# A two-layer encoder on one core: heads turned between the attention products, and half of the gated addition of rows 2 and 3 on GpSimd

## The chip, the cores and the metric

The program runs on one core of one Trainium2 chip. The metric is the device time of one execution in microseconds, the median over runs. The kernel before takes 1689.68 us (three runs, 1689.37 to 1691.24). Everything is fp32.

## The reference

Two sequences of 256 tokens (prompt and sample), 1024 wide, go through two layers and a last norm. Layer 0 mixes with latent attention, layer 1 with a gated delta rule in both directions (GDN). Both layers then have a mixture of 16 experts and a gate stage, and that stage's sum is what the next norm reads:

```python
def encoder_trunk(x, p, W):
    h = x
    for i in range(DEPTH):
        hn = rmsnorm(h, W['norm_mix_g'][i])
        j = i // N_MIXERS
        if i % N_MIXERS == 0:
            h = h + mla_mixer(hn, ...)
        else:
            h = h + gdn_mixer(hn, ...)
        h = h + expert_choice_moe(rmsnorm(h, W['norm_ffn_g'][i]), ...)
        gate = jax.nn.sigmoid(rmsnorm(h, W['norm_ple_g'][i]) @ W['ple_w_gate'][i])
        h = h + (p[i] @ W['ple_w_proj'][i]) * gate
    return rmsnorm(h, W['final_norm_g'])

def gdn_mixer(h, ...):
    ...
    o = (o_fwd + o_bwd).astype(h.dtype)
    o = rmsnorm(o, norm_g) * jax.nn.silu(z.reshape(B, S, H, GDN_DV))
    return o.reshape(B, S, H * GDN_DV) @ w_out
```

## The kernel before

The 512 tokens lie in four rows of 128 (row 0 and 1: prompt, 2 and 3: sample), kept in SBUF as `h[:, row, :]`. Each engine has one instruction stream, written by hand and worked off in order; semaphores tie the streams together. So the order of the work is the order of the code, and a wait holds back all that stands behind it on its engine.

**The gate stage**, once per layer. TensorE makes seven block products (P1, P2, P6, P5, P3, P7, P4 in this order, two row halves `t` each), from which four quarters of the product with the gate weights are put together by a scheme with seven instead of eight products. VectorE adds the products as they come out of PSUM (`gate_add`, line 3033). ScalarE takes the sigmoid of each 128x512 block (`sigmoid`, line 1456). Then the block is multiplied by the projection `pp` (line 3042) and added to `h` (line 3043): the function `gated_add(j, f)`, for row j and half f. `PLE_ORDER` fixes the eight blocks: (0,0), (1,0), (0,1), (1,1), (2,1), (3,1), (2,0), (3,0); `ple_sig` counts sigmoids, `ple_added` counts additions, both in this order. Rows 0 and 1 are done before P7; rows 2 and 3 close the stage. In `norm_quarters` ScalarE squares each half once it is added (line 951), adds a small constant (line 959), loads another table, and takes the roots (line 964); VectorE takes the reciprocal (2307) and scales (2314 in layer 0, 2310 in layer 1, where the output leaves by DMA); in layer 0 ScalarE scales the other half (line 972), and TensorE turns the rows (line 1489) for the next projection. On ScalarE the sigmoid of (2,0) stands behind the squares of (2,1), and the sigmoid of (3,0) behind the squares of (3,1) and (2,0).

**GpSimd in the gate stage** (`ple_pool`) makes sums of weight blocks for the products, four instructions of 128x2048 (lines 819, 821, 822, 825). In layer 0 the next thing in its stream is `gdn_pool`: `weight_sums(0)`, four instructions of 128x1024 on line 842 that need only weights loaded long before, and that TensorE reads after its first product of the GDN projection; then sums over the turned tokens (855, 857), which wait for TensorE and the copies out of PSUM.

**The end of the GDN mixer.** In the loop over quarters the last pass (p == QS) has on TensorE `new_values` (line 1780), `turn_heads(0)` (line 1927: heads 0 to 3 of the gated output turned, once VectorE's `gate_out(0, 2)` and `(0, 3)`, line 2777, are done), and four `attend` (line 1780), whose results VectorE adds (`add_av`, line 2766). The read of the last one frees the slots into which SyncE loads the first expert weights of layer 1 (line 662). Then come the output products (line 1499) and `turn_heads(1)`, which waits for the gated heads 4 to 7. The product P2 waits for heads 5 and 7 copied out by VectorE (line 2873).

Of the kernel before, what the change touches and what calls it, by code (L numbers as in the profile page):

```python
# [16 lines left out]
ALU = mybir.AluOpType  # L17
# [3 lines left out]
D = 1024  # L21
# [5 lines left out]
NT = SEQ // P  # L27
# [32 lines left out]
QS = 4  # L60
# [97 lines left out]
def trunk_kernel(nc, x_prompt, x_sample, p_prompt, p_sample, norm_mix_g, norm_ffn_g, norm_ple_g,  # L158
# [4 lines left out]
    with ExitStack() as ctx:  # L163
# [583 lines left out]
        def _(pool):  # L747
# [63 lines left out]
            def ple_pool(l):  # L811

                b11, b12, b21, b22 = pg_w_in(l)
                t1, t2 = pg_t(l)
                pool.wait_ge(moe_sem["w_used"], NPIECE * (l + 1))
                for f in range(2):
                    wait_use(pool, f"ple_g{f}{l}")
                pool.wait_ge(mo_tokens, PLE_TOKENS[l] + 2)
                pool.tensor_tensor(t1, b12, b11, ALU.subtract).then_inc(mo_weights, 1)  # L819
                pool.wait_ge(mo_weights, PLE_WEIGHTS[l] + 1)  # L820
                pool.tensor_tensor(t2, b22, t1, ALU.subtract).then_inc(mo_weights, 1)
                pool.tensor_tensor(b12, b22, b12, ALU.subtract).then_inc(mo_weights, 1)
                pool.wait_ge(mo_weights, PLE_WEIGHTS[l] + 3)
                pool.wait_ge(*lay[l].s_pg.full(out_no(P2, 1) + 1))
                pool.tensor_tensor(b21, b21, t2, ALU.subtract).then_inc(mo_weights, 1)

            ple_pool(0)

# [633 lines left out]
        def _(pe):  # L1462
# [209 lines left out]
            def gdn_pe():  # L1672
# [266 lines left out]
                for p in range(QS + 1):  # L1939
# [72 lines left out]
                    if live:  # L2012
                        level_turn(p, 3)
                        level_z(p, 4)
                    if p == QS:
                        turn_heads(0)
                    if p:
                        for a in range(4):
                            attend(prev, a)
                    else:  # L2020
                        gate_part(7, 5, KD)
# [273 lines left out]
        def _(dve):  # L2295
# [599 lines left out]
            for l in LAYERS:  # L2895
# [141 lines left out]
                def gated_add(j, f):  # L3037
# [2 lines left out]
                    dve.wait_ge(ple_sig, n)  # L3040
                    b, hv = ple_block(j, f), h[:, j, f * HALF:(f + 1) * HALF]
                    link(dve.tensor_tensor(b, b, pp(l)[:, j, f * HALF:(f + 1) * HALF], ALU.mult))
                    dve.tensor_tensor(hv, hv, b, ALU.add).then_inc(ple_added, 1)

                L.s_pxt.wait_read(dve, KD - 1)
# [26 lines left out]
                for t in range(NT):  # L3072
# [1 line left out]
                    gate_add(pg_q[:, t, :], pg_q[:, t, :], P7, t)  # L3074
                    dve.wait_ge(ple_added, 8 * l + 3 + t)
                    norm(normed, t)
                for t in range(NT):
                    gated_add(NT + t, 1)
                    if t == 0:
                        dve.wait_ge(*L.s_pg.freed(out_no(P7, 1)))  # L3080
                        gate_add(pg_q[:, 0, :], pg_q[:, 0, :], P4, 0)
                gated_add(NT, 0)
                gate_add(pg_q[:, 1, :], pg_q[:, 1, :], P4, 1)
                gated_add(NT + 1, 0)
# [30 lines left out]
```

## Time and profile before

| | |
|---|---|
| median of three runs | 1689.68 us |
| the profiled execution | 1692.57 us, of it span 1690.8 us |
| granted TensorE clock over the span | 0.984 |
| TensorE busy | 1590.7 us (94%) |
| VectorE, ScalarE, GpSimd busy | 674.0, 439.2, 203.6 us |
| chain that ended last | TensorE 68%, DMA 12%, VectorE 12%, ScalarE 6% |
| gate stage, layer 0 | 653.58 us to 710.26 us |
| gate stage, layer 1, with the last norm | 1631.92 us to the end |

The profile is one execution. A timeline has one row for a run of like instructions on an engine: where it starts, how long it lasts from the first start to the last end, and in brackets how long the engine was idle before it and what it was released by. An instruction's duration contains the time in which it was begun but held up. PE is TensorE, DVE VectorE, ACT ScalarE, POOL GpSimd, SP SyncE. `banks` is PSUM; `ring`, `misc`, `work`, `h`, `xn`, `xt` lie in SBUF.

### The profile page before, as it was taken

What the parts mean: (1) busy time and instruction counts of PE and PEld (TensorE: products, weight loads), DVE (VectorE), ACT (ScalarE), POOL (GpSimd) and SP (SyncE); (2) the same over time, 40 slices, a digit from 0 to 9 for tenths busy, and PEclk for the clock granted to TensorE, in tenths of its full rate; (3) what the DMA queues carried; (4) which work ended last, traced back from release to release, by engine and by line L of the source; (5) the groups of instructions that cost most, each with busy time, mean ns of one, the idle gap of its engine ahead of it and who ended that gap; (6) DMA issues with size and microseconds to landing.
All of it is one profiled execution on the core that took longest, in us unless ns stands there. A gap on an engine that the chain in (4) does not pass through costs nothing.

```text
span 1690.8 us, 21260 instructions
## 1 busy us (share of the span) xinstructions
PE 1590.7 (94%) x8950; PEld 823.3 (49%) x8950; DVE 674.0 (40%) x1130; ACT 439.2 (26%) x972; POOL 203.6 (12%) x120
## 2 busy tenths in 40 slices
PE   8989899999989978899999999998999999999887
PEld 4464534343343324488875688854344433433233
DVE  3564411131210215789983466684111312102056
ACT  4332301101101003422125765533111010110043
POOL 2302000000000004353402211130000000000021
PEclk9999999999999999999999999999999999999999
DMA  8104699999999995012121110276899999999941
GB/s 288 74 27 173 270 423 422 397 428 427 428 424 428 428 424 213 0 51 101 50 100 50 27 27 2 101 298 249 366 425 410 428 428 428 423 428 429 426 184 50
DMA packets 54045, 454.56 MB, mean 269 GB/s; under 512 B 5187, under 2 KB 7519, under 8 KB 28991
## 3 DMA queue, kind: packets, MB, share of 16 engines
q1 hardware_dynamic: 53424, 452.90, 65.3%
q8 instruction: 71, 1.16, 0.3%
q0 software_dynamic: 288, 0.22, 0.0%
q14 instruction: 23, 0.19, 0.0%
q10 hardware_dynamic: 239, 0.09, 0.0%
HBM read 451.07 MB, written 2.13 MB: 268 GB/s over the span
## 4 chain that ended last, share of the span: by engine, by line
PE 68%; DMA 12%; DVE 12%; ACT 6%; issue 2%; DVEq 0%; SPq 0%; ACTq 0%
PE banks L2151 31%; PE banks L1499 12%; DMA ring<-in_moe_w_down 7%; PE banks L2122 4%; DVE misc L2575 4%; PE banks L1682 3%; DMA ring<-in_moe_w_up 3%; PE banks L1780 3%; PE banks L2184 3%; PE banks L2212 2%; PE banks L1745 2%; DMA ring<-in_moe_w_gate 1%; PE banks L1607 1%; DVE misc L2573 1%; PE banks L2160 1%
## 5 line engine op out<-in xcount | busy, mean ns | idle before, releaser
L2151 PE MATMUL banks<-ring,misc 128*64 128x512 f32 x1984 | 442.6, 597 | 10.7 <-DMA ring<-in_moe_w_up 5.7
L2151 PEld LDWEIGHTS banks<-ring,misc 128*64 128x64 f32 x1984 | 138.7, 137 | 285.2 <-issue 266.1
L2151 PE MATMUL banks<-ring,hid_t 128*64 128x512 f32 x960 | 217.2, 605 | 14.4 <-DMA ring<-in_moe_w_down 14.3
L2999 DVE TENSOR_TENSOR work<-work,banks 128x512 f32<-128x512 f32 x32 | 33.7, 1052 | 439.9 <-PE banks L2151 439.9
L1438 ACT ACTIVATE misc<-banks 32x512 f32<-32x512 f32 x64 | 37.5, 586 | 417.2 <-PE banks L2151 416.8
L2151 PEld LDWEIGHTS banks<-ring,hid_t 128*64 128x64 f32 x960 | 69.1, 139 | 152.8 <-issue 144.0
L3014 DVE COPY misc<-banks 32x512 f32<-32x512 f32 x64 | 44.2, 691 | 229.5 <-PE banks L2151 229.1
L819 POOL TENSOR_TENSOR ring<-ring 128x2048 f32<-128x2048 f32 x2 | 10.9, 5454 | 995.0 <-DVE ring L3050 995.0
L1499 PE MATMUL banks<-ring,xt 128*128 128x512 f32 (+1 forms) x280 | 118.9, 583 | 0.2
L2575 DVE SCALAR_TENSOR_TENSOR misc<-ring,conv_w,misc 128x512 f32<-128x512 f32 x96 | 93.8, 977 | 3.4
L1682 PE MATMUL banks<-ring 128*128 128x256 f32 x384 | 86.0, 380 | 0.0
L1499 PEld LDWEIGHTS banks<-ring,xt 128*128 128x128 f32 x280 | 53.0, 190 | 63.6 <-issue 63.1
L1682 PEld LDWEIGHTS banks<-ring 128*128 128x128 f32 x384 | 72.4, 190 | 13.0 <-DVE ring L2507 3.4
L1424 ACT ACTIVATE work<-banks 128x512 f32<-128x512 f32 x32 | 19.1, 597 | 211.7 <-PE banks L2151 211.7
L842 POOL TENSOR_TENSOR ring<-ring 128x1024 f32<-128x1024 f32 x24 | 61.3, 2555 | 67.6 <-PE banks L1682 66.6
L2184 PE MATMUL banks<-misc,xt 128*128 128x512 f32 x128 | 61.8, 618 | 4.8 <-DVE misc L3014 3.4
L1682 PE MATMUL banks<-xt,ring 128*128 128x256 f32 x288 | 64.5, 380 | 0.0
L2122 PEld LDWEIGHTS banks<-xt,xn 128*128 128x128 f32 x512 | 59.5, 196 | 8.9 <-issue 6.5
L2122 PE MATMUL banks<-xt,xn 128*128 128x128 f32 x512 | 61.4, 281 | 2.2 <-DVE xt L2940 2.2
L1682 PEld LDWEIGHTS banks<-xt,ring 128*128 128x128 f32 x288 | 54.6, 190 | 7.5 <-issue 0.2
L1745 PE MATMUL banks<-ring,xt 128*128 128x512 f32 x128 | 57.5, 598 | 0.0
L1780 PE MATMUL banks<-ring 128*128 128x128 f32 x384 | 49.2, 280 | 3.9 <-DVE ring L2669 1.6
(389 smaller groups left out, 1940.0 us busy)
## 6 DMA issues: line engine op xcount, KB each, us to landing
ring<-in_moe_w_gate SPq DMA_DIRECT2D x62, 2048.0 KB, 15.5
ring<-in_moe_w_up SPq DMA_DIRECT2D x62, 2048.0 KB, 18.3
ring<-in_moe_w_down SPq DMA_DIRECT2D x56, 2048.0 KB, 19.5
ring<-in_gdn_w_in SPq DMA_DIRECT2D x8, 2048.0 KB, 8.9
ring<-in_ple_w_gate SPq DMA_DIRECT2D x4, 2048.0 KB, 16.5
ring<-in_moe_w_down SPq DMA_DIRECT2D x6, 1024.0 KB, 23.4
ring<-in_mla_w_out SPq DMA_DIRECT2D x2, 2048.0 KB, 24.3
misc<-in_moe_w_down SPq DMA_DIRECT2D x2, 2048.0 KB, 15.1
```

The costliest lines, as they stand in the source:

```text
L842: pool.tensor_tensor(out, x, y, op).then_inc(w_comb_done, 1)
L1438: ins = act.activation(ybuf[32 * i:32 * i + 32, s, 0:HALF], psum[32 * s:32 * s + 32, down_bank(ex - 1), :], ACT.Copy)
L1499: mm = pe.matmul(psum[:, banks.bank(st, i), 0:cols], lhs(k), rhs(k), start=(k == 0), stop=(k == n - 1))
L1682: mm = pe.matmul(psum[:, b, 256 * m:256 * m + 256], lhs[:, k, P * m:P * m + P], rhs[:, k, :], start=(k == 0), stop=(k == 3))
L1745: mm = pe.matmul(psum[:, apply_banks.bank(s_z, i), :], xt[:, k, j * P:(j + 1) * P], slot(6 + f, KD, HALF)[:, k, :], start=(k == 0), stop=( ...
L1780: mm = pe.matmul(o, lhs(g), rhs(g), start=True, stop=True)
L2122: mm = pe.matmul(o, xn[:, NT * s + t, c0:c0 + P], oh[:, q, NT * s + t, :], start=(t == 0), stop=(t == NT - 1))
L2151: mm = pe.matmul(psum[64 * f:64 * f + 64, bank, :], tokens(4 * kh + k), row(k, f), start=(kh == 0 and k == 0), stop=(kh == 1 and k == 3))
L2184: pe.matmul(psum[:, scatter_bank(q, g), :], sc[:, q, j, :], ybuf[:, j // NT, f * HALF:(f + 1) * HALF], start=True, stop=True).then_inc(moe ...
L2212: mm = pe.matmul(psum[:, b, :], ptt(l)[:, k, j * P:(j + 1) * P], w_proj(l)[:, k, f * HALF:(f + 1) * HALF], start=(k == 0), stop=(k == 1))
L2575: ins = dve.scalar_tensor_tensor(out=a, in0=x, scalar=w, in1=a, op0=ALU.mult, op1=ALU.add)
L3014: ins = dve.tensor_copy(ybuf[32 * i:32 * i + 32, s, HALF:D], psum[64 + 32 * s:96 + 32 * s, down_bank(ex - 1), :])
```

## The change

Two edits. First, `gated_add(2, 1)` and `gated_add(3, 1)` go from VectorE to GpSimd, in both layers, with the same arithmetic: GpSimd's multiplication waits for the sigmoid, its addition for the `ple_added` count, and VectorE's addition of (2,0) now waits until both have been counted. They are put at the end of `ple_pool`, so in layer 0 ahead of `weight_sums(0)`. On VectorE the addition of P4's first half, which stood between the two, now follows P7's norms. Second, `turn_heads(0)` goes from ahead of the four `attend` to between the second and the third.

```diff
--- before.py
+++ after.py
@@ -823,6 +823,13 @@
                 pool.wait_ge(mo_weights, PLE_WEIGHTS[l] + 3)
                 pool.wait_ge(*lay[l].s_pg.full(out_no(P2, 1) + 1))
                 pool.tensor_tensor(b21, b21, t2, ALU.subtract).then_inc(mo_weights, 1)
+                for t in range(NT):
+                    n = PLE_ORDER.index((NT + t, 1)) + 8 * l
+                    b, hv = ple_block(NT + t, 1), h[:, NT + t, HALF:D]
+                    pool.wait_ge(ple_sig, n + 1)
+                    link(pool.tensor_tensor(b, b, pp(l)[:, NT + t, HALF:D], ALU.mult))
+                    pool.wait_ge(ple_added, n)
+                    pool.tensor_tensor(hv, hv, b, ALU.add).then_inc(ple_added, 1)
 
             ple_pool(0)
 
@@ -2012,10 +2019,10 @@
                     if live:
                         level_turn(p, 3)
                         level_z(p, 4)
-                    if p == QS:
-                        turn_heads(0)
                     if p:
                         for a in range(4):
+                            if p == QS and a == 2:
+                                turn_heads(0)
                             attend(prev, a)
                     else:
                         gate_part(7, 5, KD)
@@ -3040,6 +3047,8 @@
                     dve.wait_ge(ple_sig, n)
                     b, hv = ple_block(j, f), h[:, j, f * HALF:(f + 1) * HALF]
                     link(dve.tensor_tensor(b, b, pp(l)[:, j, f * HALF:(f + 1) * HALF], ALU.mult))
+                    if (j, f) == (NT, 0):
+                        dve.wait_ge(ple_added, n - 1)
                     dve.tensor_tensor(hv, hv, b, ALU.add).then_inc(ple_added, 1)
 
                 L.s_pxt.wait_read(dve, KD - 1)
@@ -3074,11 +3083,8 @@
                     gate_add(pg_q[:, t, :], pg_q[:, t, :], P7, t)
                     dve.wait_ge(ple_added, 8 * l + 3 + t)
                     norm(normed, t)
-                for t in range(NT):
-                    gated_add(NT + t, 1)
-                    if t == 0:
-                        dve.wait_ge(*L.s_pg.freed(out_no(P7, 1)))
-                        gate_add(pg_q[:, 0, :], pg_q[:, 0, :], P4, 0)
+                dve.wait_ge(*L.s_pg.freed(out_no(P7, 1)))
+                gate_add(pg_q[:, 0, :], pg_q[:, 0, :], P4, 0)
                 gated_add(NT, 0)
                 gate_add(pg_q[:, 1, :], pg_q[:, 1, :], P4, 1)
                 gated_add(NT + 1, 0)
```

GpSimd's stream before, from the last weight sum of layer 0's gate stage on (`weight_sums` and `token_sums_dve` are counters, `slot6_loaded` is the arrival of the first GDN weights):

```order
L825 TENSOR_TENSOR ring<-ring 128x2048 [waits xt_in_psum,out_weight_sums]
L842 TENSOR_TENSOR ring<-ring 128x1024 [waits slot6_loaded,w_used]
L842 TENSOR_TENSOR ring<-ring 128x1024 [waits weight_sums] x2
L842 TENSOR_TENSOR ring<-ring 128x1024
L855 TENSOR_TENSOR ring<-xt 128x1024 [waits xt_read_dve,xt_read_act]
```

And with the change:

```order
L825 TENSOR_TENSOR ring<-ring 128x2048 [waits xt_in_psum,out_weight_sums]
L830 TENSOR_TENSOR misc<-misc,ring 128x512 [waits ple_sigmoid]
L832 TENSOR_TENSOR h<-h,misc 128x512 [waits ple_added,pool_link]
L830 TENSOR_TENSOR misc<-misc,ring 128x512 [waits ple_sigmoid]
L832 TENSOR_TENSOR h<-h,misc 128x512 [waits ple_added,pool_link]
L849 TENSOR_TENSOR ring<-ring 128x1024 [waits slot6_loaded,w_used]
L849 TENSOR_TENSOR ring<-ring 128x1024 [waits weight_sums] x2
L849 TENSOR_TENSOR ring<-ring 128x1024
L862 TENSOR_TENSOR ring<-xt 128x1024 [waits xt_read_dve,xt_read_act]
```

The four weight sums (842, now 849) stand behind four new instructions, of which the first waits for a sigmoid late in the stage.

VectorE's stream before, from the additions of P7's second half to the end of layer 0's gate stage (3033 reads PSUM, 3042 and 3043 are a gated addition):

```order
L3042 TENSOR_TENSOR misc<-misc,ring 128x512 [waits ple_sigmoid]
L3043 TENSOR_TENSOR h<-h,misc 128x512 [waits dve_link]
L3033 TENSOR_TENSOR misc<-misc,banks 128x512 [waits xt_in_psum,xt_read_dve]
L3042 TENSOR_TENSOR misc<-misc,ring 128x512 [waits ple_sigmoid]
L3043 TENSOR_TENSOR h<-h,misc 128x512 [waits dve_link]
L3042 TENSOR_TENSOR misc<-misc,ring 128x512 [waits ple_sigmoid]
L3043 TENSOR_TENSOR h<-h,misc 128x512 [waits dve_link]
L3033 TENSOR_TENSOR misc<-misc,banks 128x512 [waits xt_in_psum]
L3042 TENSOR_TENSOR misc<-misc,ring 128x512 [waits ple_sigmoid]
L3043 TENSOR_TENSOR h<-h,misc 128x512 [waits dve_link]
L2307 RECIPROCAL rstd<-rms 128x1 [waits sq_done,ple_added]
L2314 TENSOR_SCALAR xn<-h,rstd 128x512 [waits rstd_done]
```

And with the change:

```order
L3040 TENSOR_TENSOR misc<-misc,banks 128x512 [waits xt_in_psum,xt_read_dve]
L3049 TENSOR_TENSOR misc<-misc,ring 128x512 [waits ple_sigmoid]
L3052 TENSOR_TENSOR h<-h,misc 128x512 [waits ple_added,dve_link]
L3040 TENSOR_TENSOR misc<-misc,banks 128x512 [waits xt_in_psum]
L3049 TENSOR_TENSOR misc<-misc,ring 128x512 [waits ple_sigmoid]
L3052 TENSOR_TENSOR h<-h,misc 128x512 [waits dve_link]
L2314 RECIPROCAL rstd<-rms 128x1 [waits sq_done,ple_added]
L2321 TENSOR_SCALAR xn<-h,rstd 128x512 [waits rstd_done]
```

Two multiplications and two additions are gone from VectorE, and one addition has a wait more. (Lines behind the new code count seven to nine higher.)

TensorE's stream before, from the last `new_values` to the last `attend` (the rows on `misc,ring` are `attend`):

```order
L1780 MATMUL banks<-ring 128x128 [waits core_vn_read_act,gdn_ba_read_dve,core_du6_read_dve]
L1780 MATMUL banks<-ring 128x128 x3
L1927 MATMUL banks<-ident,xn 128x128 [waits gated]
L1927 MATMUL banks<-ident,xn 128x128 x15
L1780 MATMUL banks<-misc,ring 128x128 [waits core_vn_read_act,gdn_ba_t_read_dve]
L1780 MATMUL banks<-misc,ring 128x128 x3
```

And with the change:

```order
L1787 MATMUL banks<-misc,ring 128x128 [waits core_vn_read_act,gdn_ba_t_read_dve]
L1787 MATMUL banks<-misc,ring 128x128 x3
L1934 MATMUL banks<-ident,xn 128x128 [waits gated]
L1934 MATMUL banks<-ident,xn 128x128 x15
L1787 MATMUL banks<-misc,ring 128x128 [waits core_vn_read_act,gdn_ba_t_read_dve]
L1787 MATMUL banks<-misc,ring 128x128 x3
L1787 MATMUL banks<-misc,ring 128x128 [waits core_av_read_dve,gdn_ba_t_read_dve,core_vn_read_act]
L1787 MATMUL banks<-misc,ring 128x128 x3
```

The wait for the gated heads now has two `attend` less behind it. The streams of ScalarE and SyncE have the same instructions as before.

## Rows read from the trace of the kernel before

**Rows 1.** The page, part 1: busy time of each engine, and share of the span.

```profile
PE 1590.7 (94%) x8950; PEld 823.3 (49%) x8950; DVE 674.0 (40%) x1130; ACT 439.2 (26%) x972; POOL 203.6 (12%) x120
```

**Rows 2.** Timeline of VectorE, layer 0's gate: start, us, engine, line, operation, names, shapes, idle before.

```profile
676.23 2.64 DVE L3042 TENSOR_TENSOR misc<-misc,ring 128x512 f32<-128x512 f32 x1
...
684.42 2.72 DVE L3043 TENSOR_TENSOR h<-h,misc 128x512 f32<-128x512 f32 x1
...
696.93 1.28 DVE L3033 TENSOR_TENSOR misc<-misc,banks 128x512 f32<-128x512 f32 x2
...
701.01 0.69 DVE L3042 TENSOR_TENSOR misc<-misc,ring 128x512 f32<-128x512 f32 x1 [2.21 <-ACT misc L1456]
...
708.96 0.49 DVE L2314 TENSOR_SCALAR xn<-h,rstd 128x512 f32<-128x512 f32 x1
```

**Rows 3.** Timeline of GpSimd, the same stage.

```profile
672.93 5.39 POOL L825 TENSOR_TENSOR ring<-ring 128x2048 f32<-128x2048 f32 x1
678.27 11.10 POOL L842 TENSOR_TENSOR ring<-ring 128x1024 f32<-128x1024 f32 x4
```

**Rows 4.** Timeline of ScalarE, the same stage, its last part.

```profile
700.35 1.15 ACT L1456 ACTIVATE misc<-misc 128x512 f32<-128x512 f32 x2
702.46 0.63 ACT L951 ACTIVATE work<-h 128x512 f32<-128x512 f32 x1 [0.96 <-DVE h L3043]
...
703.42 0.61 ACT L1456 ACTIVATE misc<-misc 128x512 f32<-128x512 f32 x1
...
708.56 0.61 ACT L951 ACTIVATE work<-h 128x512 f32<-128x512 f32 x1
...
709.50 1.32 ACT L972 ACTIVATE xn<-h,rstd 128x512 f32<-128x512 f32 x2
```

**Rows 5.** Timeline of TensorE, the same stage.

```profile
682.29 20.76 PE L1499 MATMUL banks<-ring,xt 128*128 128x512 f32 x48
...
710.26 1.97 PE L1489 MATMUL banks<-ident,xn 128*128 128x128 f32 x8 [3.49 <-ACT xn L972]
```

**Rows 6.** Timeline of VectorE, layer 1's gate.

```profile
1675.96 1.28 DVE L2310 SCALAR_TENSOR_TENSOR xn<-h,rstd,misc 128x1024 f32<-128x1024 f32 x1
...
1681.75 0.68 DVE L3033 TENSOR_TENSOR misc<-misc,banks 128x512 f32<-128x512 f32 x1
```

**Rows 7.** Timeline of ScalarE, layer 1's gate.

```profile
1674.53 0.63 ACT L1456 ACTIVATE misc<-misc 128x512 f32<-128x512 f32 x1
...
1679.57 0.61 ACT L1456 ACTIVATE misc<-misc 128x512 f32<-128x512 f32 x1
```

**Rows 8.** Groups by line on GpSimd: count, busy us, mean ns, idle before.

```profile
L842 POOL TENSOR_TENSOR ring<-ring 128x1024 f32<-128x1024 f32 x24 | 61.3, 2555 | 67.6 <-PE banks L1682 66.6
...
L807 POOL TENSOR_TENSOR h<-h,misc 128x512 f32<-128x512 f32 x4 | 5.0, 1262 | 5.0 <-DVE misc L2450 5.0
```

**Rows 9.** Chain of waits, around the turned heads: start, us, what.

```profile
1098.34 4.74 DVE xn L2777 x8
...
1103.12 1.97 PE banks L1927 x16
1105.09 3.57 PE banks L1780 x32
...
1120.71 3.44 PE banks L1499 x8
```

**Rows 10.** Timeline of VectorE, around the turned heads.

```profile
1109.51 4.70 DVE L2777 SCALAR_TENSOR_TENSOR xn<-xn,fac,ring 128x128 f32<-128x128 f32 x4
...
1122.70 1.40 DVE L2873 TENSOR_SCALAR misc<-banks,gains 128x512 f32<-128x512 f32 x2
```

**Rows 11.** Timeline of SyncE: a weight load of layer 1's experts.

```profile
1145.07 0.33 SPq L662 DMA_DIRECT2D ring<-in_moe_w_up  x1
```

**Rows 12.** Busy us in stretches, granted clock (PEclk), DMA share and GB/s.

```profile
710.00:714.00 4.00, 3.74 (x36) 3.57 (x40) 1.69 (x3) 2.34 (x5) 0.00 (x0) 0.61 0.00 0
...
1200.00:1300.00 100.00, 99.08 (x508) 41.73 (x506) 15.38 (x26) 11.56 (x22) 0.00 (x0) 0.98 1.00 420
```

## The prediction

> **What bounds the kernel now.** I read the page's busy times first: TensorE has work for 1590.7 of 1690.8 us [rows 1], so an edit counts only where TensorE stands still, or at the very end. Three such places are touched: the end of layer 0's gate stage, the turned heads, and the last norm. I read the timeline of each engine at each of them.
>
> At the end of layer 0's gate stage TensorE is through with its products at 682.29 + 20.76 = 703.05 and starts on the rest of the turned rows only at 710.26, after an idle time put down to ScalarE [rows 5]. Between lies a chain of ScalarE and VectorE: sigmoids, gated additions, squares, roots, scaling.
>
> The decisive reading is what a GpSimd instruction does to VectorE. A gated multiplication or addition on VectorE takes 0.69 us where GpSimd is idle (701.01), and 2.64 and 2.72 us beside GpSimd's weight sums (676.23, 684.42) [rows 2]. It isn't slower work, it is waiting: the instruction of 676.23 ends at 678.87, just behind GpSimd's line 825, which ends at 678.32; and then four instructions of line 842 take 11.10 us while four of VectorE pass, so the two engines alternate in cycles of 2.78 us, some 0.68 for VectorE and 2.1 for GpSimd [rows 2, 3]. The Trainium skill states this as a rule: in "SBUF — State Buffer", section "SBUF: two separate sides", GpSimd and a VectorE instruction with two SBUF inputs take a port pair as an exclusive lock for the whole instruction, and the other is fully blocked. The trace agrees (2.64 against 0.69 us). The rule speaks against moving work to GpSimd beside a critical VectorE; that the waiting engine has its turn before the other's next instruction only the trace shows. Were the load merely shared, as the same page's section "A bandwidth-pool intuition that's wrong (but worth ruling out)" rejects, the delay would be that of my second rival.
>
> **Part 1, layer 0's gate stage.** In the kernel before, the four weight sums of line 842 run from 678.27 to 689.37 [rows 3], where VectorE has slack: the products set the pace. With the change they stand behind GpSimd's four new instructions, and these wait for a sigmoid at about 700. So the sums fall into the chain at the end. Step by step:
>
> 1. Relief early. VectorE, no longer held up at 678 to 687, gets to P7's second half when TensorE delivers it: fourth of six products in 20.76 us, so 682.29 + 4 x 3.46 = 696.13, instead of 696.93 [rows 2, 5]. Some 0.7 us. The two sigmoids of 700.35 [rows 4] start at 699.65, the first ends at about 700.3.
> 2. GpSimd's own four instructions: 128x512 additions took 1.26 us each there [rows 8]; a multiplication of that shape I take as the same. With two short hand-overs, 5.2 us: 700.35 to 705.55. The first addition ends at 702.95.
> 3. ScalarE squares (2,1) then; from the start of that square to the next sigmoid are 703.42 - 702.46 = 0.96 us [rows 4], so the sigmoid of (2,0) runs 703.95 to 704.55. Its multiplication on VectorE finds GpSimd in its fourth instruction and runs 705.6 to 706.25.
> 4. The weight sums start now. From 706.25 GpSimd and VectorE alternate: sum 1, addition of (2,0) (ends 709.0); sum 2, multiplication of (3,0) (ends 711.8, its sigmoid came at about 710.5); sum 3, addition of (3,0) (ends 714.6); sum 4 to 716.7; then the scaling of row 2, 0.49 us [rows 2], to 717.2. Before, that scaling ended at 708.96 + 0.49 = 709.45. ScalarE's part, from the square of (3,0) to its scaling 709.50 - 708.56 = 0.94 us [rows 4], fits beneath sum 4 (714.7 to 715.7).
> 5. TensorE starts on row 2 at 717.25 instead of 710.26: **+7.0 us**. It is not given back: the next stage begins with this turn. Nor does the lateness of the sums hurt there, since they end at 716.7 and TensorE needs them only after the rest of the turn and the first product.
>
> I haven't seen a GpSimd gated addition or a lock dispute over the scaling in this place; from both sides: if VectorE never lost its turn, the 0.7 gained in step 1 and the 0.5 lost in steps 2 and 3 leave -1 to +1; if it met one more cycle at each end, +9. I take 7.0, since the alternation is measured four times over.
>
> TensorE's clock: behind the 3.49 us of idle the granted clock was 0.61 over 710 to 714, so mostly at 1.2 instead of 2.4 GHz [rows 5, 12]. The idle grows to about 10.5 us. I take the same loss behind it; were it to last as long again, +1.6 us (4 x 0.39, all of it lost once more).
>
> **Part 2, the turned heads.** TensorE waits for VectorE's gating (which itself waits behind GpSimd: 4.74 us for eight small instructions) until 1103.12, with four `attend` queued behind, in the row that follows the turn, 3.57 us [rows 9]. Two of them, half of it or 1.8 us, now fill that gap. But what is late next? TensorE's product P2 starts when the turned heads 5 and 7 are copied: VectorE ends that at 1122.70 + 1.40 = 1124.10, and TensorE's own work ends at 1120.71 + 3.44 = 1124.15 [rows 9, 10]. The two are level before. So TensorE's 1.8 us is worth only what VectorE's chain gains, and that is held by GpSimd's line 911, which stretches four gatings at 1109.51 to 4.70 us [rows 10]; that instruction comes behind another on GpSimd that doesn't move, so VectorE's end moves little. I take **-0.3 us**, between 0 and -1.9. The expert weights, freed by the last `attend`, are asked for some 1.6 us earlier; it brings nothing, as five of them, 2 MB each at some 420 GB/s [rows 12], are through by about 1135, and the next load waits for an output product until 1145.07 [rows 11].
>
> From there the shift goes through one to one: the weight stream runs at full share only from 1200 on [rows 12], and what starts it is TensorE's first release of a slot.
>
> **Part 3, layer 1's gate stage and the last norm.** No weight sums follow here, only the four new instructions. GpSimd's first runs 1675.2 to 1676.45 behind the sigmoid of 1674.53 [rows 7]; VectorE's scaling of row 1, at 1675.96 [rows 6], waits for it and ends at 1677.7 (+0.4); GpSimd's addition waits in turn and ends at 1678.85, and its second pair at 1681.35. The sigmoid of (2,0), 1679.57 before [rows 7], starts at 1679.8; its multiplication waits for the lock until 1681.35, its addition ends at 1682.65, and P4's second half, 1681.75 before [rows 6], is added at 1682.6. All that follows hangs on it: **+0.9 us**, between -0.3 (P4's second half, added as soon as TensorE allows, which I put at 1681.4) and +2.
>
> **Sum.** 7.0 - 0.3 + 0.9 = +7.6 us. The profiled execution, 1692.57 us (span 1690.8), would become 1700.2. The median of the runs shown is 2.9 us lower; 1689.68 + 7.6 = **1697.3 us**, with 1695 to 1699.5 as this case's own range. From no change a measurement here can tell about 0.2%, or 3.4 us.
>
> **Rivals.**
> - *The gate is delayed further* (0.12): the alternation meets more VectorE instructions, or the low clock behind the longer idle lasts. +9 or +7.6 + 1.6, near 1699.5 to 1701.
> - *Little dispute at the end* (0.14): the weight sums fall into gaps where VectorE waits for ScalarE anyway. For: VectorE itself waits there for ScalarE, 2.21 us before 701.01 [rows 2]. Against: cycles of 2.78 us four times running. It costs 1 to 3 us, 1691 to 1692.5.
> - *Faster* (0.05): the lock falls to VectorE at each of its requests at 705 to 717, and VectorE's gating of the heads also comes out ahead of line 911. Then the early relief (-0.7) and two `attend` in TensorE's gap (-1.9) remain, -0.3 at the end: 1689.68 - 2.9 = 1686.8. It decides for this case if VectorE's gated additions keep 0.69 us at the end of layer 0's stage. Against it stands that GpSimd's instruction, once begun, wasn't interrupted anywhere in rows 2 and 3.
> - The forecast: 0.69.
>
> Eight times in ten: 1692.0 to 1700.5. Faster by over 0.2% is a part of the third rival alone, 0.03; slower by over 0.2% (above 1693.1) is the forecast and the first rival, and a little of the second, 0.82; the rest, 0.15, within.
>
> **What would show it.** Line 849 (the weight sums) for the first four times at 706 to 717 instead of 678 to 689; beside it VectorE's lines 3049 and 3052 of 2 to 2.8 us; TensorE's idle before the turn of row 2 grown from 3.5 to 10 us or more. At 678 to 687 VectorE's gated additions at 0.7 us. At the heads, the idle before `attend` gone but P2 at the same distance. If line 849's instructions run there and VectorE keeps its 0.69 us, step 4 is wrong; if TensorE's idle stays at 3.5 us, all of part 1 is.

## The result and the profile after

The changed kernel takes 1694.54 us (median of nine runs, 1692.03 to 1703.15) against 1689.68 us of the kernel before beside it (nine runs, 1685.64 to 1693.54): ratio 1.0035, 95% interval 1.0021 to 1.0050, so 5.9 us longer, 3.5 to 8.4 (the medians alone differ by 4.9 us). The forecast was 1697.3 us with slower as the likeliest; the median lies in the range for eight times in ten (1692.0 to 1700.5), and 0.5 us below the forecast's own case (1695 to 1699.5). The profiled execution took 1697.51 us (span 1695.6), before 1692.57 (1690.8).

The page's first part, the line that answers to [rows 1]:

```profile
PE 1590.4 (94%) x8950; PEld 824.0 (49%) x8950; DVE 672.3 (40%) x1122; ACT 439.3 (26%) x972; POOL 214.5 (13%) x128
```

TensorE's work hasn't changed; it stands still for longer. To see where, I cut the program at points that both kernels have on TensorE (and, at the end, VectorE's last scaling) and compared the distances between them. As a single execution scatters, both kernels were profiled twice more, and the table has the mean of three profiles each (the values apart where they matter):

| stretch | before | after | difference |
|---|---|---|---|
| start to the gate products, P3 (ahead of the change) | 681.90 | 681.26 | -0.6 |
| P3 to the turn of row 2, layer 0 | 27.97 (27.96 to 27.98) | 33.80 (33.79 to 33.80) | **+5.8** |
| turn of row 2 to the last `new_values` | 384.10 (386.16, 383.32, 382.81) | 384.02 (384.60, 382.98, 384.48) | -0.1 |
| last `new_values` to P2 of layer 1 (the turned heads) | 27.49 (27.78, 27.79, 26.89) | 27.30 (27.60, 27.09, 27.22) | **-0.2** |
| P2 to P3, layer 1 (experts and gate products) | 536.12 (536.44, 536.52, 535.41) | 537.73 (537.24, 538.02, 537.94) | +1.6 |
| P3, layer 1, to the end of the last scaling | 27.14 (27.14 to 27.15) | 27.88 (27.88 to 27.90) | **+0.7** |

They add up to the difference of the mean spans, 7.3 us. The three bold rows are those in which the change has its instructions: +6.4 us, where the prediction had +7.6. The last number for the heads is smaller than their scatter; it is measured more sharply below.

**Layer 0's gate.** TensorE's timeline of the changed kernel:

```profile
681.37 20.76 PE L1506 MATMUL banks<-ring,xt 128*128 128x512 f32 x48
...
715.17 1.97 PE L1496 MATMUL banks<-ident,xn 128*128 128x128 f32 x8 [5.92 <-ACT xn L979]
```

From the end of the last product (681.37 + 20.76 = 702.13) to row 2's turn are now 13.0 us instead of 7.2 [rows 5]. VectorE's timeline there:

```profile
677.97 0.69 DVE L3052 TENSOR_TENSOR h<-h,misc 128x512 f32<-128x512 f32 x1
...
703.68 1.49 DVE L3049 TENSOR_TENSOR misc<-misc,ring 128x512 f32<-128x512 f32 x1 [4.19 <-ACT misc L1463]
705.21 2.71 DVE L3052 TENSOR_TENSOR h<-h,misc 128x512 f32<-128x512 f32 x1
...
709.23 1.45 DVE L3049 TENSOR_TENSOR misc<-misc,ring 128x512 f32<-128x512 f32 x1 [0.71 <-ACT misc L1463]
710.71 2.71 DVE L3052 TENSOR_TENSOR h<-h,misc 128x512 f32<-128x512 f32 x1
...
713.53 2.38 DVE L2321 TENSOR_SCALAR xn<-h,rstd 128x512 f32<-128x512 f32 x1
```

And GpSimd's:

```profile
699.44 1.27 POOL L830 TENSOR_TENSOR misc<-misc,ring 128x512 f32<-128x512 f32 x1 [22.06 <-ACT misc L1463]
...
703.37 1.26 POOL L832 TENSOR_TENSOR h<-h,misc 128x512 f32<-128x512 f32 x1
704.58 11.05 POOL L849 TENSOR_TENSOR ring<-ring 128x1024 f32<-128x1024 f32 x4
```

VectorE's additions early in the stage, which took 2.72 us beside the sums [rows 2], take 0.69 us (677.97), as GpSimd stands idle then. The price is paid at the end: the four weight sums run from 704.58 to 715.63, and VectorE's additions of (2,0) and (3,0) and its scaling take 2.71, 2.71 and 2.38 us instead of 0.69, 0.69 and 0.49 [rows 2]. ScalarE's last part, which answers to [rows 4]:

```profile
714.41 0.71 ACT L979 ACTIVATE xn<-h,rstd 128x512 f32<-128x512 f32 x1
```

ScalarE ends its half of row 2 at 715.12 and TensorE starts at 715.17, while VectorE's scaling runs until 715.91. ScalarE's half alone releases the turn.

**The heads.** TensorE's timeline around the turned heads (it answers to [rows 9]):

```profile
1103.69 1.95 PE L1787 MATMUL banks<-misc,ring 128*128 128x128 f32 x16
1106.58 1.97 PE L1934 MATMUL banks<-ident,xn 128*128 128x128 f32 x16 [0.93 <-DVE xn L2784]
1108.38 1.95 PE L1787 MATMUL banks<-misc,ring 128*128 128x128 f32 x16
...
1127.37 1.10 PE L1506 MATMUL banks<-ring,misc 128*128 128x512 f32 x2 [0.74 <-issue]
```

VectorE's, which answers to [rows 10]:

```profile
1111.97 5.41 DVE L2784 SCALAR_TENSOR_TENSOR xn<-xn,fac,ring 128x128 f32<-128x128 f32 x4
...
1125.87 1.41 DVE L2880 TENSOR_SCALAR misc<-banks,gains 128x512 f32<-128x512 f32 x2
```

And GpSimd's row beside the first of these:

```profile
1112.08 4.63 POOL L918 TENSOR_TENSOR ring<-xt,ring 128x2048 f32<-128x2048 f32 x1
```

Two `attend` fill the gap at 1103.69, and TensorE is through earlier; but it then stands idle for 0.74 us until 1127.37. The row names no releaser, but the start falls right behind the end of VectorE's copy, 1125.87 + 1.41. VectorE is held as before by GpSimd's long instruction, now for 5.41 us over four small ones (4.70 before).

What this is worth can't be read from the stretch as a whole: it takes 26.89 to 27.79 us in the three profiles of the kernel before. The scatter comes from eight gatings of VectorE that lie ahead of the turned heads, beside GpSimd's line 906. First profile of the kernel before, VectorE's row and then GpSimd's:

```profile
1098.26 4.81 DVE L2777 SCALAR_TENSOR_TENSOR xn<-xn,fac,ring 128x128 f32<-128x128 f32 x8
1096.55 4.53 POOL L906 TENSOR_TENSOR xt<-xt 128x2048 f32<-128x2048 f32 x1
```

Its second repeat:

```profile
1094.45 3.92 DVE L2777 SCALAR_TENSOR_TENSOR xn<-xn,fac,ring 128x128 f32<-128x128 f32 x8
1091.84 4.54 POOL L906 TENSOR_TENSOR xt<-xt 128x2048 f32<-128x2048 f32 x1
```

The GpSimd instruction ends 2.82 us behind the first gating's start in the one and 1.93 in the other, and the gatings take 0.89 us less. Counted from the end of these eight gatings to P2 the scatter is gone: 21.13 us in all five profiles, of any kernel here, that have the turn at its old place, and 20.84 to 20.86 in all seven that have it moved and nothing else changed at the heads. The moved turn gains 0.28 us.

**The last norm.** GpSimd's four instructions in layer 1:

```profile
1679.21 1.27 POOL L830 TENSOR_TENSOR misc<-misc,ring 128x512 f32<-128x512 f32 x1 [18.57 <-ACT misc L1463]
1680.56 2.13 POOL L832 TENSOR_TENSOR h<-h,misc 128x512 f32<-128x512 f32 x1
1682.65 1.26 POOL L830 TENSOR_TENSOR misc<-misc,ring 128x512 f32<-128x512 f32 x1
1683.99 1.26 POOL L832 TENSOR_TENSOR h<-h,misc 128x512 f32<-128x512 f32 x1
```

And VectorE's scaling of row 1 and its multiplication of (2,0):

```profile
1679.94 1.62 DVE L2317 SCALAR_TENSOR_TENSOR xn<-h,rstd,misc 128x1024 f32<-128x1024 f32 x1
...
1684.33 1.48 DVE L3049 TENSOR_TENSOR misc<-misc,ring 128x512 f32<-128x512 f32 x1 [1.59 <-ACT misc L1463]
```

Here each engine waits for the other: the scaling takes 1.62 instead of 1.28 us, the GpSimd addition 2.13 instead of 1.26, and the multiplication 1.48 instead of 0.68.

### The profile page after: what moved, and what is told of

Same layout as the page of the kernel before. It is cut to its first block and busy times, and to the rows that moved or that the text cites. A ratio compares the mean times of both kernels' runs of the same rounds, so it can differ in the third digit from the quotient of the medians.

```text
span 1695.6 us, 21266 instructions
## 1 busy us (share of the span) xinstructions
PE 1590.4 (94%) x8950; PEld 824.0 (49%) x8950; DVE 672.3 (40%) x1122; ACT 439.3 (26%) x972; POOL 214.5 (13%) x128
## 3 DMA queue, kind: packets, MB, share of 16 engines
HBM read 451.07 MB, written 2.13 MB: 267 GB/s over the span
```

## The experiments

All ratios are to the kernel before, run beside the experiment on the same chip. A pause is the time from the end of P3 and what is joined to it (its start + 20.76 us) to TensorE's turn of row 2: 7.2 us before, 13.0 after. "Heads" is the distance from the last `new_values` to P2, "gatings to P2" that from the end of the eight gatings, "tail" that from layer 1's P3 to the last scaling's end.

**The turn alone.** Kernel before with

```diff
-                    if p == QS:
-                        turn_heads(0)
                     if p:
                         for a in range(4):
+                            if p == QS and a == 2:
+                                turn_heads(0)
                             attend(prev, a)
```

> The kernel before with the turned heads between the second and third attend, and nothing on GpSimd moved. My theory: TensorE's pause ahead of the turn shrinks from 2.6 us to about 0.8 us, but product P2 starts only 0.1 to 0.4 us earlier relative to the last new_values, because it waits for VectorE's copy of heads 5 and 7; the time is that of before, within 0.05% (ratio 0.999 to 1.000). Rival (the filled pause is worth its full length): P2 starts 1.8 us earlier, ratio 0.9989.

Ratio 0.9999 (0.9987 to 1.0012). Pause 7.2, heads 27.56, tail 27.15 us. TensorE's idle time ahead of the turned heads fell from 2.6 to 0.9 us, but gatings to P2 is 20.85 for 21.13: of the 1.8 us that the gap takes in, 0.28 come out. That is too little to be told in the time.

**The GpSimd part alone.** The changed kernel with the same edit undone.

> The changed kernel with the turned heads back ahead of the four attend; GpSimd's gated additions stay. My theory: all of the loss is here. In layer 0 TensorE starts on the rest of row 2 about 12.2 us after its last gate product, as in the changed kernel (before: 7.2 us), and the last norm ends 0.7 us later relative to P3's start; the ratio is that of the changed kernel, 1.0035, within 0.001. Rival (the moved turn costs something too): ratio clearly below that of the changed kernel, 1.001 to 1.002.

Ratio 1.0045 (1.0029 to 1.0062). Pause 13.06, heads 28.02 (gatings to P2 21.13), tail 27.90 us. All of the loss is in this part. (The 12.2 us that this expectation and the next give for the changed kernel are 13.0 by the measure used here.)

**The sums first.** The changed kernel, with layer 0's gated additions behind the weight sums in GpSimd's stream:

```diff
                 weight_sums(0)
+                ple_adds(0)
```

(`ple_adds` holds the four new instructions, called at the old place for layer 1 only.)

> The changed kernel, with layer 0's four weight sums for the GDN projection put ahead of GpSimd's gated additions again, so that they run at about 678 to 689 us as before. My theory (the loss in layer 0 comes from the sums that fell into the end of the stage): beside the last gated additions of VectorE there is only GpSimd's own fourth instruction; TensorE starts on the rest of row 2 about 8.5 us after its last gate product (before 7.2, changed kernel 12.2), and the time is some 4 us below the changed kernel's, ratio to before about 1.001. Rival (the four instructions on GpSimd cost the time themselves, being 1.26 against 0.69 us and one more engine in the chain): 11 to 12 us after the last product, ratio near 1.003.

Ratio 1.0016 (1.0002 to 1.0030). VectorE's timeline:

```profile
705.23 1.48 DVE L3055 TENSOR_TENSOR misc<-misc,ring 128x512 f32<-128x512 f32 x1 [4.86 <-ACT misc L1469]
706.75 0.69 DVE L3058 TENSOR_TENSOR h<-h,misc 128x512 f32<-128x512 f32 x1
```

Pause 9.0 us, tail 27.90. With the sums back in their old place the addition takes 0.69 us again, and 4.0 of the 5.8 us are gone, though the relief early in the stage (0.7 us) is lost with them. The pause was expected at 8.5 us. What stays, 1.8 us, is the price of GpSimd's own four instructions: 5.2 us in line where VectorE needed four times 0.69, and one multiplication held for 0.8 us.

**The sums late, on the kernel before.** The counterpart: all gated additions stay on VectorE, and only the sums move to the end.

```diff
                 pool.wait_ge(moe_sem["w_used"], NPIECE)
+                pool.wait_ge(ple_sig, 6)
                 weight_sums(0)
```

> The kernel before with a single edit: layer 0's four weight sums wait for the sigmoid of (3,1); all gated additions stay on VectorE. My theory (it is the place of the sums, not GpSimd's gated additions): VectorE's additions at the end of the stage take 2 to 2.8 us, and TensorE starts on the rest of row 2 some 14.5 to 15 us after its last gate product (before 7.2, changed kernel 13.0); ratio 1.003 to 1.006. Rival (the loss needs the gated additions on GpSimd): 7 to 9 us, ratio within 0.001 of 1.

Ratio 1.0028 (1.0010 to 1.0046). VectorE's timeline, one row for each gated instruction from (2,1)'s multiplication to (2,0)'s addition:

```profile
700.81 0.69 DVE L3043 TENSOR_TENSOR misc<-misc,ring 128x512 f32<-128x512 f32 x1 [2.21 <-ACT misc L1457]
701.54 2.79 DVE L3044 TENSOR_TENSOR h<-h,misc 128x512 f32<-128x512 f32 x1
...
704.85 2.24 DVE L3043 TENSOR_TENSOR misc<-misc,ring 128x512 f32<-128x512 f32 x1
707.12 2.71 DVE L3044 TENSOR_TENSOR h<-h,misc 128x512 f32<-128x512 f32 x1
709.76 2.82 DVE L3043 TENSOR_TENSOR misc<-misc,ring 128x512 f32<-128x512 f32 x1
712.62 0.69 DVE L3044 TENSOR_TENSOR h<-h,misc 128x512 f32<-128x512 f32 x1
```

GpSimd's row beside them:

```profile
701.43 10.60 POOL L842 TENSOR_TENSOR ring<-ring 128x1024 f32<-128x1024 f32 x4 [22.63 <-issue]
```

Pause 14.3 us (14.5 or more was expected). Four sums, four VectorE instructions held up, 1.6 to 2.1 us each; the fifth, at 712.62, is free again. So the place of the sums alone, with no work moved to GpSimd, makes the loss and a little more. Between this run and the one above, the main cause is shown from both sides.

**The sums in halves.** The changed kernel, with each of the four sums as two instructions of 128x512:

```diff
+                        if u == 0:
+                            pool.tensor_tensor(out[:, 0:2, :], x[:, 0:2, :], y[:, 0:2, :], op)
+                            pool.tensor_tensor(out[:, 2:4, :], x[:, 2:4, :], y[:, 2:4, :], op).then_inc(w_comb_done, 1)
+                            return
```

> The changed kernel, with each of layer 0's four weight sums at the end of the gate stage made by two instructions of half the size. My theory (a VectorE instruction waits for one whole GpSimd instruction): VectorE's lines 3049 and 3052 there wait for half as long, 1.7 us instead of 2.7 for the longest; TensorE starts on the rest of row 2 some 10.7 us after its last gate product instead of 13.0; ratio about 1.002. Rival (the two engines share the access and slow each other by the amount of work): 13 us as before, or a little more, since the work is the same.

Ratio 1.0018 (1.0004 to 1.0031). VectorE's timeline:

```profile
704.29 1.64 DVE L3056 TENSOR_TENSOR h<-h,misc 128x512 f32<-128x512 f32 x1
...
710.72 1.30 DVE L2325 TENSOR_SCALAR xn<-h,rstd 128x512 f32<-128x512 f32 x1
```

Pause 11.1 us, for an expected 10.7. The additions take 1.64 instead of 2.71, the scaling 1.30 instead of 2.38 us: so the wait in front of VectorE's own 0.69 us fell from 2.0 to 0.95, in half like the size of the GpSimd instruction. A load that is merely shared would not care how it is cut. Each of these VectorE instructions waits for one whole GpSimd instruction and no more.

**The sums after the stage.** The changed kernel, with the sums held until row 3 is scaled:

```diff
                 pool.wait_ge(moe_sem["w_used"], NPIECE)
+                for s in (xn_act, xn_dve):
+                    pool.wait_ge(s, NJ * norm_no["mix1"])
                 weight_sums(0)
```

> The changed kernel, with GpSimd waiting, before layer 0's four weight sums, until row 3 has been scaled; so they run behind the gate stage. My theory: VectorE's gated additions at the end of the stage take 0.7 us but for the one beside GpSimd's fourth instruction, TensorE starts on the rest of row 2 about 8 us after its last gate product; the sums then hold up VectorE's sums over the turned tokens, and product P6 of the GDN projection starts up to 2 us later relative to the turn; ratio 1.0005 to 1.002. Rival (sums needed so early that TensorE waits for them): P6 4 us or more later relative to the turn, ratio as the changed kernel's or above.

Ratio 1.0084 (1.0061 to 1.0108): slower than the changed kernel, against my expectation. The pause did fall, to 8.3 us. But from the turn of row 2 to the last `new_values` it takes 392.6 us, where all others here take 381.4 to 388.0. GpSimd's timeline behind the turn:

```profile
709.97 11.38 POOL L849 TENSOR_TENSOR ring<-ring 128x1024 f32<-128x1024 f32 x4 [6.54 <-ACT xn L981]
...
725.90 3.51 POOL L868 MEMSET xn<- 128x4096 f32 x1
729.49 7.18 POOL L849 TENSOR_TENSOR ring<-ring 128x1024 f32<-128x1024 f32 x3
```

VectorE's small instructions beside them:

```profile
721.47 2.27 DVE L2549 SCALAR_TENSOR_TENSOR fac<-fac 128x64 f32<-128x64 f32 x1
724.30 5.15 DVE L2553 TENSOR_SCALAR fac<-fac 128x64 f32<-128x64 f32 x1 [0.57 <-ACT alog L1155]
725.93 3.56 DVE L2554 TENSOR_SCALAR fac<-fac 128x64 f32<-128x64 f32 x1
...
731.92 2.41 DVE L2560 SCALAR_TENSOR_TENSOR fac<-fac 128x64 f32<-128x64 f32 x1
734.37 2.35 DVE L2561 TENSOR_SCALAR fac<-fac 128x64 f32<-128x64 f32 x1
```

And TensorE's row that waits for their result:

```profile
737.03 1.92 PE L1718 MATMUL banks<-fac,tri 128*128 128x32 f32 x8 [6.64 <-DVE fac L2562]
```

All that GpSimd does behind the sums comes later, and so lies beside the short chain in which VectorE forms the decay factors, instructions of some 0.2 us each, of which five now take 2.3 to 5.2 us. (Three of that chain took 2.4 to 2.6 us before as well.) TensorE waits for it until 27.8 us behind the turn of row 2 (737.03 - 709.28), with 6.64 us of idle time; before it had no wait there, at 20.9 us (731.12 - 710.26). That is 6.9 us, and 2.8 more follow: behind the idle time the granted clock is 0.63 from 737.0 to 744.5, and the same products that took 4.4 us before take 7.2. From 35 us behind the turn on TensorE is 9.7 us late, against the 4.7 us that the pause gave back. I had looked only at whether TensorE would be kept waiting for the sums; it wasn't (its products with them start at 719.86, 10.6 us behind the turn, 10.5 before). The dispute moved to the next chain of VectorE, and there it was dearer.

**GpSimd's line 911 behind the gating.** The prediction held that this instruction is what limits the gain at the heads. Kernel before with the turn moved, and:

```diff
                 pool.wait_ge(*core["av"].full(16))
+                pool.wait_ge(gated, 2 * NJ)
                 pool.tensor_tensor(go_t2, go_b22, go_t1, ALU.subtract).then_inc(mo_weights, 1)
```

> The turned heads moved as in the changed kernel, no gated additions on GpSimd, and GpSimd's 128x2048 sum on line 911 (918 in the changed kernel) now waits until all heads are gated. My theory: P2 waits for VectorE, whose gating of heads 4 to 7 waits for that one GpSimd instruction; without it the four gatings of the first row take 1.1 instead of 4.7 us, and P2 starts about 1.8 us earlier behind the last new_values than with the moved turn alone. Ratio 0.9985 to 0.9995. Rival (VectorE is paced by ScalarE's roots there): P2 starts less than 0.5 us earlier.

Ratio 0.9971 (0.9955 to 0.9987), so faster than before; median 1686.79 us. VectorE's timeline:

```profile
1104.61 1.14 DVE L2778 SCALAR_TENSOR_TENSOR xn<-xn,fac,ring 128x128 f32<-128x128 f32 x4
1106.44 0.18 DVE L2775 RECIPROCAL fac<-fac 128x4 f32<-128x4 f32 x1 [0.70 <-ACT fac L1279]
```

The four gatings take 1.14 instead of 4.70 us, and the next limit shows: the reciprocal waits for ScalarE's root, 0.70 us in each of the three rounds that follow. Heads 25.88 us, gatings to P2 19.13: 1.7 us less than with the turn alone (20.85) and 2.0 less than before (21.13). The ratio is worth 4.9 us (2.2 to 7.6), more than these 2.0; its pause (7.2) and tail (27.15) are those of before, so the rest must lie in stretches that scatter (below), and I don't ascribe it to the edit.

**Both places.** The same kernel with, in layer 0, the addition of P4's first half ahead of `gated_add(2, 1)`:

```diff
+                if l == 0:
+                    dve.wait_ge(*L.s_pg.freed(out_no(P7, 1)))
+                    gate_add(pg_q[:, 0, :], pg_q[:, 0, :], P4, 0)
                 for t in range(NT):
                     gated_add(NT + t, 1)
```

(The same addition between the two, further down, is then for layer 1 only.)

> As the run with line 911 waiting for the gated heads, and in layer 0 VectorE adds P4's first half ahead of the gated addition of (2,1), which still waits for its sigmoid then. My theory: 0.2 us more in layer 0; ratio 0.998 to 0.9995, the fastest of all. Rival (nothing of it reaches the end): ratio 1.000.

Ratio 0.9980 (0.9964 to 0.9996), median 1687.23 us. Pause 6.98 instead of 7.21 us, heads 25.47, gatings to P2 19.13 again. The step is there in the profile and can't be told apart in the time: that this kernel is the fastest of all isn't shown. Both of these kernels are faster than the kernel before: their intervals lie wholly below 1.

**Repeats.** In the first pair of profiles the stretch from the turn of row 2 to the last `new_values` was 1.6 us shorter after than before, as if something were given back. Both kernels were profiled twice more, unedited, under these expectations (changed kernel, then kernel before):

> The changed kernel once more, one profile, nothing edited. Question: from TensorE's turn of row 2 (end of layer 0's gate stage) to the start of the last 32 matmuls on new values ahead of the turned heads the profile of before has 386.2 us and that of the changed kernel 384.6, though no instruction of that stretch is changed. Theory (the placing of TensorE's low-clock stretches differs from one execution to the next): the distance in this profile differs from 384.6 by 1 us or more in one at least of two repeats of the changed kernel. Rival (the later weight sums on GpSimd really shorten the stage): 384.6 within 0.5 us in both. Pause before row 2's turn 13.0 within 0.3, heads 27.6 within 0.3, tail 27.9 within 0.1 by either.

> Second repeat of the changed kernel, as the first. Theory: the distance from row 2's turn to the last new values scatters over 381.9 to 387.5, which four kernels with the same stretch have shown. Rival: 384.6 within 0.5.

> The kernel before once more, one profile, nothing edited. Theory (scatter of the low-clock stretches): the same distance, 386.2 in its first profile, differs by 1 us or more in one at least of two repeats. Rival (it belongs to the kernel): 386.2 within 0.5 in both. Pause 7.2 and tail 27.15 by either.

> Second repeat of the kernel before, as the third run. Theory: distance anywhere in 381.9 to 387.5. Rival: 386.2 within 0.5.

The changed kernel gave 382.98 and 384.48 us, the kernel before 383.32 and 382.81 after a first 386.16. One program differs from itself by 3.3 us, and the means are level. More sharply: TensorE's products at 731.12 in the first profile of the kernel before stand 20.86 us behind the turn of row 2, and those that answer to them stand there within 0.01 us in each of these six profiles. So nothing is given back where the sums could have done it. The pauses were 13.0, 13.0, 7.2 and 7.2 us, the tails 27.90, 27.88, 27.15 and 27.14: what the first edit touches repeats within 0.05 us. One miss: the heads, which I had put at 27.6 within 0.3 by either, gave 27.09 and 27.22. They scatter with the place of GpSimd's line 906 (913 in the changed kernel), as shown above; gatings to P2 is 20.85 and 20.84 in the two.

## Why the prediction was right, and where it was off

**Step 1, the relief.** Right. Counted from P3's start (0.92 us earlier in this profile, before anything changed), the sigmoids start at 698.73 for 699.65 - 0.92. It is the same number.

**Steps 2 and 3, GpSimd's four instructions.** Right: 699.44 to 704.63 is 5.2 us, and the multiplication is 1.27 where I had taken the addition's 1.26. VectorE's multiplication of (2,0) ends at 705.17; predicted, with the same 0.92 off, 705.33. Only the detail was off: it began before GpSimd's last instruction was through, and the first sum came behind it.

**Step 4, the alternation.** Right, and shown by three runs: taken away with the sums (9.0 us of pause), made by the sums alone (14.3), halved with their size (11.1). The sums end at 715.63 for a predicted 715.8.

**Step 5, +7.0 us.** The size was off: +5.8, and the same 5.83 in three profiles. I let TensorE wait for VectorE's scaling, the last event of my list, and put that end at 716.3, counted from this profile's P3 (it was 715.91). But the turn begins with the half that ScalarE scales, and that is ready 0.8 us sooner, at 715.12. [Rows 5] had said so: the idle before the turn is put down to ScalarE's line 972, at 710.26, when VectorE's scaling had been through since 709.45. I had read the row for its length and not for its releaser. My own step 4 had ScalarE's part done at 715.7, but that was a misreading too: the 0.94 us run from the start of the square to the start of the scaling (708.56 to 709.50), and TensorE started 0.76 us behind that. With it TensorE would have started at 716.4, +6.1. Nearly all of the remaining 0.3 us is VectorE's addition of (3,0), which ended at 713.42 for a predicted 713.7. One sign that I had named failed: TensorE's idle before the turn of row 2 is 5.92 us and not 10 or more. The pause holds two idle stretches, since two other matmuls stand between, at 706.33 before and 708.57 now; they were 1.75 and 3.49 us and are 4.91 and 5.92, and I had put the whole delay on the second.

**TensorE's clock.** I took the same loss behind the longer idle. Over the 4 us behind the turn of row 2 the granted clock was 0.65, 0.57 and 0.50 in the three profiles of the kernel before, and 0.50, 0.59 and 0.50 in those of the changed kernel: mostly 1.2 GHz in both, and no lower for the longer idle. Nor does it matter there, as TensorE soon stands idle for VectorE again. Before:

```profile
720.59 0.33 PE L1516 MATMUL banks<-ident,work 128*128 128x128 f32 x1 [1.03 <-DVE work L2321]
```

After:

```profile
725.50 0.33 PE L1523 MATMUL banks<-ident,work 128*128 128x128 f32 x1 [0.69 <-DVE work L2328]
```

Both stand 10.33 us behind their turn (710.26 and 715.17), and so do the rows that answer to them in the other profiles, within 0.01 us, but for the run with the sums after the stage (10.41). What the low clock costs ahead of this wait is swallowed by it. So the term of the rival, +1.6 us, was zero, and I had named no reason for it to reach the end.

**Part 2, -0.3 us.** Right: -0.28 (gatings to P2, 20.85 against 21.13, whichever kernel has the turn moved); the stretch as a whole would not have shown it. That VectorE and TensorE were level before was the reading that decided it, and the run that held GpSimd's instruction back shows the reason as well: once VectorE is free of it, 1.7 us more come out. The earlier expert loads brought nothing that shows.

**Part 3, +0.9 us.** Right in mechanism and nearly in size: P4's second half is added 0.73 us later, counted from P3 (0.85 predicted), and the end comes with it: +0.74, and the same 0.75 in each kernel that has the four instructions on GpSimd (tail 27.88 to 27.90), while those without have 27.14 to 27.15.

**What I had not in the sum.** From P2 to P3 of layer 1 the three profiles after are 1.6 us longer. No instruction there is changed. What differs is the granted clock in the 35 us from 40 us behind P2 on. The window in the second repeat of the kernel before:

```profile
1159.50:1194.50 35.00, 30.73 (x223) 16.88 (x225) 10.98 (x31) 7.72 (x13) 0.00 (x0) 1.00 0.80 323
```

And in the first repeat of the changed kernel:

```profile
1166.15:1201.15 35.00, 31.31 (x211) 18.14 (x213) 10.70 (x30) 7.73 (x13) 0.00 (x0) 0.90 0.73 291
```

The third number from the end is the granted clock: 1.00 in the one, 0.90 in the other. Over all profiles this window shows three values: with 1.00 the whole from P2 to P3 took 535.3 and 535.4 us, with 0.95 536.0 to 538.8, with 0.90 537.7 to 539.7. So the clock is a part of it and not all. The seven profiles of kernels without GpSimd's additions had 0.95 or 1.00 and took 535.3 to 538.8 us, which covers the three after (537.2 to 538.0). Yet all four with 0.90 are kernels that have these additions, as are three of those with 0.95. Whether the change has a part in the 1.6 us is open; I count them as scatter. That the spans differ by 7.3 us, so near the predicted 7.6, is therefore in part luck: the three stretches without an instruction of the change add 0.9 us to the 6.4, about what the sum had too much.

The rivals: little dispute at the end (0.14) fell with the rows of 2.71 us; the further delay (0.12) with the pause of 13.0. Of the rival that would have made it faster, each condition can be read: VectorE's gated additions did not keep their 0.69 us, and the gating did not come ahead of GpSimd's line 918. The experiments that take the dispute away come near to it: with the sums first 4.0 us of the pause come back (not all, and the kernel is still no faster than before), and with GpSimd's instruction held back 1.7 us come out at the heads.

## What to carry to other kernels

Before an elementwise instruction goes to GpSimd, list which of VectorE's instructions on SBUF, those with two inputs and `TENSOR_SCALAR` (the scaling here, 2.38 for 0.49 us), will lie beside it and beside everything that it pushes back in GpSimd's stream; on a chain that TensorE waits for, each can cost the whole GpSimd instruction in front of it. It is cheaper to leave GpSimd's bulk work where another engine sets the pace, or to cut it small, than to shift it to where the next chain stands, as the run with the sums after the stage shows. And end a sum at the releaser that the row names, not at the last event of your own list.

## What the runs showed of the hardware

- The two engines take turns: four GpSimd sums of 128x1024 with a VectorE instruction between each take 11.05 us in the changed kernel, 10.60 in the run with the sums late on the kernel before, and 11.10 at their old place [rows 3]. In these rows VectorE is held by one GpSimd instruction: 2.71 us for 0.69 beside 128x1024, 1.64 beside 128x512.
- I had not expected that very small instructions pay the same. A 128x64 `TENSOR_SCALAR` on SBUF, some 0.2 us by itself, took 2.35 us beside a sum, and two of them 5.15 and 3.56 us until GpSimd's `MEMSET`, which reads nothing, was through at 729.41. The first of the two, begun at 724.30, was held by two GpSimd instructions in a row: the sum over the turned tokens that ended at 725.96, and then the `MEMSET`. So that VectorE always has its turn after one GpSimd instruction holds for the gated additions and not for every instruction; the runs don't show why. The Trainium skill ("SBUF — State Buffer", section "Who interferes with whom") lists `tensor_scalar` among those that can take both ports and so contend with GpSimd. The trace agrees. A 128x64 `SCALAR_TENSOR_TENSOR` was not held by the `MEMSET`: 0.22 us at 722.58 in the kernel before, beside the `MEMSET` of 722.41 to 725.92, where the `TENSOR_SCALAR` of 723.38 took 2.59.
- The instructions of VectorE that read PSUM were not lengthened in any row that I read: 0.67 us at 707.84 in the changed kernel's `gate_add`, beside a GpSimd sum (707.45 to 710.13).
- TensorE's low-clock stretches fall on other work from one execution to the next of the same program. The 384 us of the GDN mixer differ by 3.3 us among three profiles of the kernel before (386.16, 383.32, 382.81), more than the whole effect of the second edit, and the granted clock over their last quarter goes with it (0.91, 0.95, 0.96).
